# Every fourth low weight part of feed-forward made by an adding DMA instead of by VectorE

## The chip, the cores and the metric

The kernel runs on one core of one Trainium2 chip. The metric is the device time of one execution in microseconds; the time before is the median of three runs.

## The reference

A decoder block over 256 tokens of width 2048, all in float32: a conditioning vector gives shifts, scales and gates; a normalised and modulated input goes through one wide projection into gated linear attention (4 heads) and forgetting attention (16 heads), whose outputs are projected, gated, merged and added to x. The part that the change touches is the last:

```python
h2 = rms_norm(x, g_norm2[l]) * (1.0 + scale2) + shift2
x = x + gate2 * (jnp.square(jax.nn.relu(h2 @ w_ff1[l])) @ w_ff2[l])
return rms_norm(x, g_final)
```

with `w_ff1` of 2048 x 8192 and `w_ff2` of 8192 x 2048.

## The kernel before, in words

**Arithmetic.** A float32 product is made from three products in the format fp32r: each factor is split into a high part (itself, rounded) and a low part (what the rounding left out), and TensorE sums high x high, high x low and low x high. For the weights the high part `whi` is a copy by ScalarE that rounds (`hi`, L691 to L701), and the low part `wlo` is a subtraction by VectorE, raw minus `whi` (`lo`, L1156 to L1162).

**Units.** The weights are cut into units of 128 partitions x 2 x 512 float32, 512 KB. There are 608; `UNITS` (L59) numbers them in the order of their use. The sections are the three of the head, those of forgetting attention, of linear attention, of the mixing, of the output projection, and from `G_FF` = 352 on feed-forward: 256 units in four quarters (`it`) of 64, in each 32 units of `up` and 32 of `down`. `token_unit` (L1728) does one unit on TensorE: for two blocks of 128 tokens and two slices of the contraction three matmuls each, 12 in all, L1741.

**Buffers.** `raw` is a ring of 5 (`RING`), filled by DMAs that SP issues (`load`, L553; the issue is L577). Besides the units of the weights, pieces of `w_ada` ride in this ring up to the first part of feed-forward (L568). `whi` and `wlo` are rings of 4 (`WRING`), so that units of equal index modulo 4 share a buffer (`parts`, L505). All queues are written out by hand. In step g each of ScalarE and VectorE works on unit g + 3 (`LEAD`; `ahead`, L204).

**Semaphores.** ScalarE rounds unit g when its load has landed and TensorE has done unit g - 4 (`s_pe`), and raises `s_hi`. VectorE waits for `s_hi`, subtracts and raises `s_lo`, by one for each unit. TensorE waits for `s_lo` at g + 1 before the first matmul of unit g (L1731); SP waits for the same count before it loads into the raw buffer that unit g has left (L560).

**Other work in feed-forward.** In steps 8, 16, 24 and 32 of a quarter ScalarE takes a finished block out of PSUM with a relu (L1044) and VectorE squares it; in steps 11, 19, 27 and 35 TensorE transposes it by eight small matmuls (`turn`, L1717 to L1726); in steps 12, 20, 28 and 36 ScalarE and VectorE split it into its high and low part (L1050, L1586). VectorE adds the results of `down` to the residual stream (L1532, L1536).

**GpSimd.** It makes constants at the start, issues eight small DMAs of 4 and 8 KB (L645, L646), and computes the powers of the norms (L633, L637, L652). The last two powers (L652) belong to the final norm.

Of the kernel before, what the change touches and what calls it, by code (L numbers as in the profile page):

```python
# [6 lines left out]
ALU = mybir.AluOpType  # L7
# [186 lines left out]


NORM2_UNITS = (4, 9, 14)

# [32 lines left out]
def build(nc, x, c, w_ada, b_ada, g_norm1, w_in, w_gla_a_up, b_gla_a, g_gla_out, b_fox_f,  # L232
# [181 lines left out]

    s_hi = nc.alloc_semaphore("s_hi")
    s_lo = nc.alloc_semaphore("s_lo")
    s_pe = nc.alloc_semaphore("s_pe")
    s_bank = nc.alloc_semaphore("s_bank")
    s_bk = [nc.alloc_semaphore(f"s_bk{i}") for i in range(6)]
# [85 lines left out]
    def parts(g):  # L505

        if G_LAST <= g < NG - WRING:
            return hi_last[g - G_LAST], lo_last[g - G_LAST]
        return whi[g % WRING], wlo[g % WRING]
# [19 lines left out]
    with nc.Block() as block:  # L529


        @block.sync
        def _(sp):

            def load_bias(ag, col):
                if ag:
                    sp.wait_ge(s_ada, pieces_done(ag - 1, 0))
                for h in range(2):
                    sp.dma_start(bi[32 * h:32 * h + 1, :], b_ada[0:1, col + h * NB:col + h * NB + NB]).then_inc(s_bi, 16)

            def load_first(p):
                n, k = PIECE[p]
                col = n % 2 * 2 * NB + (D if n < 2 else 0)
                if p == P_0[n]:
                    if n:
                        sp.wait_ge(s_ada, 2 * (P_0[n - 1] + 1))
                    sp.dma_start(bih[0:1, :], b_ada[0:1, col:col + 2 * NB]).then_inc(s_bih, 16)
                if p >= FRING:
                    sp.wait_ge(s_ada, 2 * (p - FRING + 1))
                    sp.wait_ge(s_adp, pieces_pe(p - FRING))  # L550
                sp.dma_start(first[p % FRING][:], w_ada_v[:, k, col:col + 2 * NB]).then_inc(s_fraw[p % FRING], 16)

            def load(pos):  # L553
                kind, what = STREAM[pos]
                if kind == "a" and what[1] == 0:
                    load_bias(what[0], ADA_COL[what[0]])
                if pos >= RING:
                    kind_, what_ = STREAM[pos - RING]
                    if kind_ == "g":
                        sp.wait_ge(s_lo, what_ + 1)  # L560
                    elif kind_ == "w":
                        sp.wait_ge(s_wacc, 2 * what_ + 2)
                    else:
                        sp.wait_ge(s_ada, pieces_done(*what_))
                r = raw[pos % RING]
                if kind == "a":
                    m, k = what
                    sp.dma_start(r[:].rearrange("p k n -> p (k n)"), w_ada_v[:, k, ADA_COL[m]:ADA_COL[m] + 2 * NB]  # L568
                                 ).then_inc(s_raw[pos % RING], 16)
                elif kind == "w" and what >= UG:  # L570
                    both = w_in_v[:, what - UG, C_GV:C_GV + 2 * (C_GG - C_GV)].rearrange("p (a n) -> p a n", a=2)
                    sp.dma_start(r[:], both[:, :, 0:NB]).then_inc(s_raw[pos % RING], 16)
                else:
                    parts = source(what if kind == "g" else UNIT[("fq", 0), what])
                    n = NB // len(parts)
                    for a, src in enumerate(parts):
                        sp.dma_start(r[:, :, a * n:a * n + n], src).then_inc(s_raw[pos % RING], 16)  # L577

            sp.dma_start(x_in[:], x_v).then_inc(s_x, 16)
            sp.wait_ge(s_init, 1)  # L580
            loaded = 0
            for p in range(PIECES):
                load_first(p)
                while loaded < LOADED[p]:
                    load(loaded)
                    loaded += 1
            for pos in range(loaded, len(STREAM)):
                if pos == G_FOX + 4:

                    sp.wait_ge(s_zero, 1)  # L590
                    sp.dma_start(small[:, :, 0:RANK], w_in_v[:, :, C_LOW:C_LOW + RANK]).then_inc(s_small, 16)
                    sp.dma_start(small[:, :, 32:32 + FH], w_in_v[:, :, C_FL:C_FL + FH]).then_inc(s_small, 16)  # L592
                load(pos)

            for t in range(TT):
                for h, done in enumerate((s_ya, s_yo)):
                    half = slice(h * (D // 2), (h + 1) * (D // 2))
                    sp.wait_ge(done, t + 1 if h == 0 else 2 * t + 2)
                    sp.dma_start(out_v[:, t, half], xl[:, t, half]).then_inc(s_out, 16)
            sp.wait_ge(s_out, 16 * 2 * TT)  # L600


        @block.gpsimd
        def _(pool):
            nc.gpsimd.memset(bih[:], 0.0).then_inc(s_init, 1)
            nc.gpsimd.memset(ident[:], 0.0)
            nc.gpsimd.memset(ones[:], 1.0).then_inc(s_ones, 1)
            nc.gpsimd.memset(neghalf[:], -0.5)
            nc.gpsimd.memset(mhi[:], BIG)
            nc.gpsimd.memset(mlo[:], -BIG)  # L610
            nc.gpsimd.memset(tri[:], 1.0)
            nc.gpsimd.memset(tri16[:], 1.0 / TAU)
            nc.gpsimd.memset(fm[:], 0.0)
            nc.gpsimd.memset(am[:], 0.0)
            nc.gpsimd.memset(gl[:], 1.0).then_inc(s_init, 1)
            pool.wait_ge(s_init, 2)

            nc.gpsimd.affine_select(out=ident[:], in_=ident[:], compare_op=ALU.not_equal, fill=1.0, base=0,
                                    pattern=[[-1, P]], channel_multiplier=1).then_inc(s_ident, 1)
            nc.gpsimd.memset(small[:], 0.0).then_inc(s_zero, 1)  # L620
            for t_ in (mhi, mlo, tri, tri16):
                nc.gpsimd.affine_select(out=t_[:], in_=t_[:], compare_op=ALU.is_ge, fill=0.0, base=0,
                                        pattern=[[1, P]], channel_multiplier=-1).then_inc(s_mask, 1)
            for b in (0, 2):
                nc.gpsimd.affine_select(out=fm[:, b * P:b * P + P], in_=fm[:, b * P:b * P + P],
                                        compare_op=ALU.is_ge, fill=-1e30, base=0,
                                        pattern=[[-1, P]], channel_multiplier=1).then_inc(s_mask, 1)
            pool.wait_ge(s_mask, 6)
            nc.gpsimd.memset(tri16[0:CH, CH:P], 0.0).then_inc(s_mask, 1)

            def norm_pow(r):
                pool.wait_ge(s_nms, r + 1)
                nc.gpsimd.tensor_tensor(nst[:, 2, :], nst[:, 1, :], neghalf[:], ALU.pow).then_inc(s_ny, 1)  # L633

            def gla_pow(h):
                pool.wait_ge(s_gms, h + 1)
                nc.gpsimd.tensor_tensor(nst[:, 2, :], nst[:, 1, :], neghalf[:], ALU.pow).then_inc(s_gy, 1)  # L637

            norm_pow(0)

            pool.wait_ge(s_fcd, 4)
            for a in range(2):
                own = slice(a * FH // 2, (a + 1) * FH // 2)
                for row, src in ((32 * a, nch), (32 * a + 1, ncl)):
                    nc.gpsimd.dma_start(ncrow[row:row + 1, :, 0:P], src[own, 0:P]).then_inc(s_rowcum, 16)  # L645
                    nc.gpsimd.dma_start(ncrow[row:row + 1, :, P:3 * P], src[own, :]).then_inc(s_rowcum, 16)  # L646
            for h in range(4):
                gla_pow(h)
            norm_pow(1)
            for t in range(TT):  # L650
                pool.wait_ge(s_nms, 3 + t)
                nc.gpsimd.tensor_tensor(nst[:, 2, t:t + 1], nst[:, 1, t:t + 1], neghalf[:, 0:1], ALU.pow  # L652
                                        ).then_inc(s_ny, 1)
# [3 lines left out]
        def _(act):  # L657
# [33 lines left out]
            def hi(g):  # L691

                if g >= NG:
                    return
                act.wait_ge(s_raw[POS_G[g] % RING], landed(POS_G[g]))
                if g >= NG - WRING:

                    act.wait_ge(s_pe, g - 2 * WRING + 1)
                elif g >= WRING and g < G_LAST:
                    act.wait_ge(s_pe, g - WRING + 1)  # L700
                nc.scalar.activation(parts(g)[0][:], raw[POS_G[g] % RING][:], ACT.Copy).then_inc(s_hi, 1)  # L701

            act.wait_ge(s_nr, 3)
            nc.scalar.activation(xn[:, 1, :], x_in[:, 1, :], ACT.Copy, scale=nst[:, 5, 1:2]).then_inc(s_xna, 1)
# [370 lines left out]
        def _(dve):  # L1075
# [79 lines left out]

            def lo(g):  # L1156

                if g >= NG:
                    return
                dve.wait_ge(s_hi, g + 1)  # L1160
                top, rest = parts(g)
# [470 lines left out]
        def _(pe):  # L1632
# [95 lines left out]
            def token_unit(name, u, src, ready=None, rows=range(TT)):  # L1728
                g = UNIT[name, u]
                top, rest = parts(g)  # L1730
                pe.wait_ge(s_lo, g + 1)  # L1731
                for t in rows:
                    if u == 0:
                        bank_free(name, t)
# [339 lines left out]
```

## Time and profile before

| | us |
|---|---|
| median of three runs | 1881.63 |
| lowest and highest | 1879.43, 1885.69 |
| span of the profiled execution | 1879.2 |
| TensorE busy in it | 1835.8 |
| VectorE busy | 1231.8 |
| ScalarE busy | 848.2 |
| GpSimd busy | 17.7 |

Of the profiled execution the span from the first to the last instruction is given, and no time of its own beside it. PE is TensorE, PEld its loads of the stationary operand, DVE VectorE, ACT ScalarE, POOL GpSimd; SPq is the queue of SyncE that issues DMAs. Busy time of an engine says how much it works, not whether anybody waits for it; for that there are the waits and the chain that ended last.

### The profile page before, as it was taken

What the parts mean: (1) busy time and instruction counts of PE and PEld (TensorE: products, weight loads), DVE (VectorE), ACT (ScalarE), POOL (GpSimd) and SP (SyncE); (2) the same over time, 40 slices, a digit from 0 to 9 for tenths busy, and PEclk for the clock granted to TensorE, in tenths of its full rate; (3) what the DMA queues carried; (4) which work ended last, traced back from release to release, by engine and by line L of the source; (5) the groups of instructions that cost most, each with busy time, mean ns of one, the idle gap of its engine ahead of it and who ended that gap; (6) DMA issues with size and microseconds to landing.
All of it is one profiled execution on the core that took longest, in us unless ns stands there. A gap on an engine that the chain in (4) does not pass through costs nothing.

```text
span 1879.2 us, 21671 instructions
## 1 busy us (share of the span) xinstructions
PE 1835.8 (98%) x8351; PEld 1485.1 (79%) x8351; DVE 1231.8 (66%) x1368; ACT 848.2 (45%) x1075; POOL 17.7 (1%) x40
## 2 busy tenths in 40 slices
PE   6998999999999999999999998999999999999998
PEld 3666888888888888888888886888888888888886
DVE  6996666666666667666576777775555555555555
ACT  4444545455544554344444444443444344434443
POOL 1000000000000000000000000000000000000000
PEclk8999999999999999999999998999999999999999
DMA  9998899899997987998899784886666666666663
GB/s 382 399 318 250 215 218 278 240 232 256 206 206 236 214 246 232 250 260 295 276 256 266 254 282 156 286 279 201 192 190 180 194 198 181 190 192 191 188 190 123
DMA packets 214767, 441.50 MB, mean 235 GB/s; under 512 B 18437, under 2 KB 34917, under 8 KB 214282
## 3 DMA queue, kind: packets, MB, share of 16 engines
q1 hardware_dynamic: 213272, 436.57, 78.5%
q10 hardware_dynamic: 1138, 3.50, 0.5%
q8 instruction: 67, 1.10, 0.2%
q14 instruction: 34, 0.28, 0.0%
q0 software_dynamic: 256, 0.05, 0.0%
HBM read 437.92 MB, written 2.10 MB: 234 GB/s over the span
## 4 chain that ended last, share of the span: by engine, by line
PE 89%; DVE 2%; DMA 1%; issue 1%; SPq 1%; ACT 0%; POOL 0%; POOLq 0%; DVEq 0%
PE ps L1741 82%; PE ps L1725 1%; DMA raw<-in_w_in 1%; PE ps L1845 1%; DVE wlo L1162 1%; DVE acch L1134 0%; SPq L592 0%; PE ps L1897 0%; PE ps L1649 0%; PE ps L1651 0%; DVE xT L1567 0%; PE ps L1842 0%; ACT whi L701 0%; PE ps L1854 0%; DVE obT L1571 0%
## 5 line engine op out<-in xcount | busy, mean ns | idle before, releaser
L1162 DVE TENSOR_TENSOR wlo<-raw,whi 128x1024 fp32r<-128x1024 f32 x604 | 738.3, 1224 | 587.4 <-ACT whi L701 585.3
L701 ACT ACTIVATE whi<-raw 128x1024 fp32r<-128x1024 f32 x604 | 639.5, 1060 | 935.9 <-PE ps L1741 719.3
L1741 PE MATMUL ps<-whi,hT 128*128 128x512 f32 x2304 | 742.9, 397 | 5.0 <-DVE wlo L1162 4.6
L1741 PEld LDWEIGHTS ps<-whi,hT 128*128 128x128 f32 x2304 | 435.1, 189 | 114.0 <-DVE wlo L1162 13.1
L1741 PE MATMUL ps<-wlo,hT 128*128 128x512 f32 x1152 | 450.6, 391 | 0.0
L1741 PE MATMUL ps<-whi,obT 128*128 128x512 f32 x1280 | 403.9, 393 | 3.9 <-DVE wlo L1162 2.7
L1741 PE MATMUL ps<-whi,oaT 128*128 128x512 f32 x1248 | 389.0, 390 | 0.0
L1741 PEld LDWEIGHTS ps<-whi,obT 128*128 128x128 f32 x1280 | 242.0, 189 | 56.3 <-DVE wlo L1162 4.2
L1741 PEld LDWEIGHTS ps<-whi,oaT 128*128 128x128 f32 x1248 | 234.3, 188 | 48.9 <-issue 0.5
L1741 PEld LDWEIGHTS ps<-wlo,hT 128*128 128x128 f32 x1152 | 217.7, 189 | 45.4 <-issue 2.2
L1741 PE MATMUL ps<-wlo,obT 128*128 128x512 f32 x640 | 250.5, 391 | 0.0
L1741 PE MATMUL ps<-wlo,oaT 128*128 128x512 f32 x624 | 242.8, 389 | 0.0
L1273 DVE SCALAR_TENSOR_TENSOR acc<-raw,cond,acc 128x1024 f32<-128x1024 f32 x120 | 153.3, 1277 | 0.7 <-DMA raw<-in_w_ada 0.4
L1741 PEld LDWEIGHTS ps<-wlo,obT 128*128 128x128 f32 x640 | 121.1, 189 | 25.1 <-issue 0.5
L1741 PEld LDWEIGHTS ps<-wlo,oaT 128*128 128x128 f32 x624 | 117.2, 188 | 24.6 <-issue 0.5
L1134 DVE SCALAR_TENSOR_TENSOR acch<-first,cond,acch 128x1024 f32<-128x1024 f32 (+1 forms) x60 | 64.1, 1068 | 8.5 <-DMA first<-in_w_ada 5.1
L1532 DVE TENSOR_TENSOR rt<-ps,gate 128x512 f32<-128x512 f32 x40 | 27.4, 684 | 8.4 <-PE ps L1741 8.4
L1699 PE MATMUL ps<-first,cond 128*1 128x512 f32 x48 | 26.9, 660 | 4.1 <-DMA first<-in_w_ada 4.1
L1536 DVE TENSOR_TENSOR xl<-xl,rt 128x512 f32<-128x512 f32 x40 | 27.7, 693 | 4.2
L1580 DVE TENSOR_TENSOR t<-t 128x512 f32<-128x512 f32 x32 | 20.6, 684 | 0.0
L1586 DVE TENSOR_TENSOR oaT<-ps,oaT 128x512 fp32r<-128x512 f32 x32 | 20.5, 682 | 0.0
L1225 DVE SCALAR_TENSOR_TENSOR accv<-raw,modc,accv 128x1024 f32<-128x1024 f32 x15 | 19.1, 1275 | 0.0
(234 smaller groups left out, 783.7 us busy)
## 6 DMA issues: line engine op xcount, KB each, us to landing
raw<-in_w_ff SPq DMA_DIRECT2D x256, 512.0 KB, 4.2
raw<-in_w_in SPq DMA_DIRECT2D x248, 512.0 KB, 6.7
raw<-in_w_ada SPq DMA_DIRECT2D x128, 512.0 KB, 5.2
first<-in_w_ada SPq DMA_DIRECT2D x64, 512.0 KB, 10.2
raw<-in_w_in SPq DMA_DIRECT2D x64, 256.0 KB, 6.1
raw<-in_w_proj_fox SPq DMA_DIRECT2D x32, 512.0 KB, 5.7
raw<-in_w_proj_gla SPq DMA_DIRECT2D x32, 512.0 KB, 5.6
raw<-in_w_out SPq DMA_DIRECT2D x32, 512.0 KB, 5.0
```

The costliest lines, as they stand in the source:

```text
L701: nc.scalar.activation(parts(g)[0][:], raw[POS_G[g] % RING][:], ACT.Copy).then_inc(s_hi, 1)
L1134: V.scalar_tensor_tensor(b[:, c], a[:, c], cond[:, k:k + 1], bih[:] if k == 0 else b[:, c], ALU.mult, ALU.add).then_inc(s_ada, 2)
L1162: V.tensor_tensor(rest[:], raw[POS_G[g] % RING][:], top[:].bitcast(F32), ALU.subtract).then_inc(s_lo, 1)
L1225: V.scalar_tensor_tensor(acc_, w, col, acc_, ALU.mult, ALU.add).then_inc(s_wacc, inc)
L1273: V.scalar_tensor_tensor(acc[:], raw[pos % RING][:].rearrange("p k n -> p (k n)"), cond[:, k:k + 1], acc[:], ALU.mult, ALU.add).then_inc(s ...
L1532: V.tensor_tensor(rt[:, t, :], ps[bank(name, t)][:], gate[:, cols], ALU.mult).then_inc(s_bk[bank(name, t)], 1)
L1536: V.tensor_tensor(xl[:, t, cols], xl[:, t, cols], rt[:, t, :], ALU.add).then_inc(s_x2, 1)
L1580: V.tensor_tensor(t5[:, t, :], t5[:, t, :], t5[:, t, :], ALU.mult).then_inc(s_act, 1)
L1586: V.tensor_tensor(oaT[:, 4 * b:4 * b + 4, 1, t * P:t * P + P], ps[bank(("up", n), t)][:].rearrange("p (k n) -> p k n", k=4), oaT[:, 4 * b: ...
L1699: T.matmul(ps[6][0:1, :], cond[:, k:k + 1], first[p % FRING][:, 0:NB], start=(p == p0), stop=(p == p1)).then_inc(s_adp, 1)
L1725: i = T.transpose(ps[bank(name, t)][:, k * P:k * P + P], src[:, t, k * P:k * P + P], ident[:])
L1741: i = T.matmul(ps[bank(name, t)][:], src[:, kt, hl, tk], w[:, k, :], start=(kt == 0 and n == 0), stop=(kt == KT - 1 and n == 2))
```

## The change

For every fourth unit of feed-forward (unit numbers that leave 2 when divided by 4, from 358 to 590) ScalarE makes, behind the rounded copy, a second one with scale -1, which it writes into the unit's `wlo` buffer. GpSimd waits for it and issues a DMA that reads the unit's weights from memory again and adds them onto that buffer, which then holds the raw value minus the rounded one. VectorE leaves these units out. TensorE waits for the DMA's semaphore in these units, and for a count of `s_lo` that leaves them out in the others; SP takes the raw buffer of such a unit as free after the negated copy.

```diff
--- before.py
+++ after.py
@@ -194,6 +194,21 @@
 
 
 NORM2_UNITS = (4, 9, 14)
+
+
+
+FOLD = [g for g in range(G_FF + 6, NG - 2 * UG) if g % 4 == 2]
+FOLD_N = {g: n for n, g in enumerate(FOLD)}
+
+
+def folded(g):
+
+    return sum(f <= g for f in FOLD)
+
+
+def own_lo(g):
+
+    return g + 1 - folded(g)
 
 
 
@@ -414,6 +429,8 @@
 
     s_hi = nc.alloc_semaphore("s_hi")
     s_lo = nc.alloc_semaphore("s_lo")
+    s_neg = nc.alloc_semaphore("s_neg")
+    s_fold = nc.alloc_semaphore("s_fold")
     s_pe = nc.alloc_semaphore("s_pe")
     s_bank = nc.alloc_semaphore("s_bank")
     s_bk = [nc.alloc_semaphore(f"s_bk{i}") for i in range(6)]
@@ -557,7 +574,10 @@
                 if pos >= RING:
                     kind_, what_ = STREAM[pos - RING]
                     if kind_ == "g":
-                        sp.wait_ge(s_lo, what_ + 1)
+                        if what_ in FOLD_N:
+                            sp.wait_ge(s_neg, FOLD_N[what_] + 1)
+                        else:
+                            sp.wait_ge(s_lo, own_lo(what_))
                     elif kind_ == "w":
                         sp.wait_ge(s_wacc, 2 * what_ + 2)
                     else:
@@ -647,6 +667,9 @@
             for h in range(4):
                 gla_pow(h)
             norm_pow(1)
+            for n, g in enumerate(FOLD):
+                pool.wait_ge(s_neg, n + 1)
+                nc.gpsimd.dma_start(parts(g)[1][:], source(g)[0], accum_op=ALU.add).then_inc(s_fold, 16)
             for t in range(TT):
                 pool.wait_ge(s_nms, 3 + t)
                 nc.gpsimd.tensor_tensor(nst[:, 2, t:t + 1], nst[:, 1, t:t + 1], neghalf[:, 0:1], ALU.pow
@@ -699,6 +722,8 @@
                 elif g >= WRING and g < G_LAST:
                     act.wait_ge(s_pe, g - WRING + 1)
                 nc.scalar.activation(parts(g)[0][:], raw[POS_G[g] % RING][:], ACT.Copy).then_inc(s_hi, 1)
+                if g in FOLD_N:
+                    nc.scalar.activation(parts(g)[1][:], raw[POS_G[g] % RING][:], ACT.Copy, scale=-1.0).then_inc(s_neg, 1)
 
             act.wait_ge(s_nr, 3)
             nc.scalar.activation(xn[:, 1, :], x_in[:, 1, :], ACT.Copy, scale=nst[:, 5, 1:2]).then_inc(s_xna, 1)
@@ -1155,7 +1180,7 @@
 
             def lo(g):
 
-                if g >= NG:
+                if g >= NG or g in FOLD_N:
                     return
                 dve.wait_ge(s_hi, g + 1)
                 top, rest = parts(g)
@@ -1728,7 +1753,10 @@
             def token_unit(name, u, src, ready=None, rows=range(TT)):
                 g = UNIT[name, u]
                 top, rest = parts(g)
-                pe.wait_ge(s_lo, g + 1)
+                if g in FOLD_N:
+                    pe.wait_ge(s_fold, 16 * (FOLD_N[g] + 1))
+                else:
+                    pe.wait_ge(s_lo, own_lo(g))
                 for t in rows:
                     if u == 0:
                         bank_free(name, t)
```

## Rows read from the trace of the kernel before

**Rows 1.** The page: busy time, and the busy tenths of 40 slices.

```profile
PE 1835.8 (98%) x8351; PEld 1485.1 (79%) x8351; DVE 1231.8 (66%) x1368; ACT 848.2 (45%) x1075; POOL 17.7 (1%) x40
...
PE   6998999999999999999999998999999999999998
...
DVE  6996666666666667666576777775555555555555
ACT  4444545455544554344444444443444344434443
```

**Rows 2.** The page: the chain that ended last, by line.

```profile
PE ps L1741 82%; PE ps L1725 1%; DMA raw<-in_w_in 1%; PE ps L1845 1%; DVE wlo L1162 1%; DVE acch L1134 0%; SPq L592 0%; PE ps L1897 0%; PE ps L1649 0%; PE ps L1651 0%; DVE xT L1567 0%; PE ps L1842 0%; ACT whi L701 0%; PE ps L1854 0%; DVE obT L1571 0%
```

**Rows 3.** Stretches of feed-forward: us, busy (count) by engine, granted clock, DMA share, GB/s.

```profile
1190.00:1250.00 60.00, 60.00 (x274) 49.86 (x273) 43.77 (x43) 28.25 (x34) 0.00 (x0) 1.00 0.83 276
...
1400.00:1600.00 200.00, 200.00 (x904) 166.04 (x903) 109.91 (x108) 86.05 (x92) 0.00 (x0) 1.00 0.64 189
```

**Rows 4.** 1190 to 1850 us: waits (total, times, longest), then groups of instructions.

```profile
ACT whi L701 <- PE ps L1741: 368.9, 231, 2.6
DVE wlo L1162 <- ACT whi L701: 273.0, 212, 2.4
ACT whi L701 <- DMA raw<-in_w_ff: 4.0, 3, 2.1
...
L1162 DVE TENSOR_TENSOR wlo<-raw,whi 128x1024 fp32r<-128x1024 f32 x235 | 287.9, 1225 | 273.1 <-ACT whi L701 273.0
L701 ACT ACTIVATE whi<-raw 128x1024 fp32r<-128x1024 f32 x236 | 250.2, 1060 | 373.0 <-PE ps L1741 368.9 <-DMA raw<-in_w_ff 4.0
```

**Rows 5.** Timeline from 1500 us: start, us, engine, line, operation [idle before].

```profile
1500.12 0.19 PEld L1741 LDWEIGHTS ps<-wlo,oaT 128*128 128x128 f32 x1
1500.34 0.39 PE L1741 MATMUL ps<-wlo,oaT 128*128 128x512 f32 x1
...
1500.57 0.62 PE L1741 MATMUL ps<-whi,oaT 128*128 128x512 f32 x2
...
1501.05 1.06 ACT L701 ACTIVATE whi<-raw 128x1024 fp32r<-128x1024 f32 x1 [1.66 <-PE ps L1741]
...
1502.14 1.23 DVE L1162 TENSOR_TENSOR wlo<-raw,whi 128x1024 fp32r<-128x1024 f32 x1 [1.50 <-ACT whi L701]
...
1503.77 1.06 ACT L701 ACTIVATE whi<-raw 128x1024 fp32r<-128x1024 f32 x1 [1.66 <-PE ps L1741]
...
1508.73 0.62 PE L1741 MATMUL ps<-whi,oaT 128*128 128x512 f32 x2
```

**Rows 6.** Timeline of ACT: a rounding and what runs directly behind it.

```profile
1536.41 1.06 ACT L701 ACTIVATE whi<-raw 128x1024 fp32r<-128x1024 f32 x1 [1.66 <-PE ps L1741]
1537.38 1.07 ACT L1044 ACTIVATE t<-ps 128x512 f32<-128x512 f32 x2
```

**Rows 7.** Loads of L577, 1400 to 1850 us, and the page's DMA totals.

```profile
DMA to landing us min/median/max: 3.6/3.9/6.0
...
DMA packets 214767, 441.50 MB, mean 235 GB/s; under 512 B 18437, under 2 KB 34917, under 8 KB 214282
```

**Rows 8.** POOL's timeline, and the landing of its small DMAs (tile ncrow).

```profile
208.18 0.52 POOL L646 DMA_DIRECT2D ncrow<-nch  x1
...
1143.72 0.69 POOL L633 TENSOR_TENSOR nst<-nst,neghalf 128x2 f32<-128x2 f32 x1 [413.29 <-DVE nst L1114]
1861.67 0.55 POOL L652 TENSOR_TENSOR nst<-nst,neghalf 128x1 f32<-128x1 f32 x1 [717.26 <-DVE nst L1114]
...
DMA to landing us min/median/max: 3.2/3.8/4.0
```

**Rows 9.** All DMA issues: KB each, median us to landing.

```profile
raw<-in_w_in SPq DMA_DIRECT2D x248, 512.0 KB, 6.7
```

**Rows 10.** DMA in the first 50 us: GB/s of 40 slices.

```profile
GB/s 0 97 244 419 420 432 397 419 419 419 413 410 403 400 419 416 413 403 393 419 395 400 400 395 398 398 410 398 405 392 401 406 397 400 410 383 393 415 405 388
```

**Rows 11.** The chain from 1480 to 1560 us: start, us, what.

```profile
1544.48 0.87 PE ps L1725 x8
```

## The prediction

> **What bounds the kernel now.** I read the views from the coarse to the fine. First the page's busy shares and its 40 slices [rows 1]: TensorE is busy 98% of the span and VectorE 66%; the reader is to see that in the last 15 slices, feed-forward, PE stays at 9 while DVE falls to 5 and ACT is at 3 to 4. Then the chain that ended last [rows 2]: 82% of the span is the weight matmuls of L1741, while the low parts of L1162 are near 0%. Then the stretches of feed-forward [rows 3]: PE is busy in every microsecond (PE's column equals the length of the stretch) at a granted clock of 1.00, which is the 2.4 GHz level. Then the waits there [rows 4]: DVE waits 273.0 us for ACT's rounded part, ACT waits 368.9 us for PE to free a buffer, and PE waits for no other engine. So VectorE's work in this stage is off the path. Taking it away cannot shorten anything by itself; the question is only whether the new way delivers each low part in time.
>
> **How much time a low part has.** One unit is 12 matmuls. In the timeline [rows 5] the rounding activations start at 1501.05 and 1503.77, so a unit lasts 2.72 us. The pair of matmuls at 1500.57 is the last of one unit and the first of the next, the second of them starting 0.23 later, at 1500.80 (its end at 1500.96, 0.09 before the activation, is what releases ACT). The buffer freed there serves the unit three places behind the one just begun, whose first matmul is the second of the pair at 1508.73, that is 1508.96; a stationary load starts 0.22 ahead of its matmul (1500.12 and 1500.34), and it stands behind the same wait. So from 1501.05 the low part has until 1508.74, 7.7 us. Today it needs 2.3: 1.06 for ACT, 1.23 for DVE until 1503.37 [rows 5]. That leaves 5.4 us unused.
>
> **The change part by part.**
> *Count.* The changed units run from feed-forward's sixth to before its last sixteen, every fourth: 59.
> *Removed:* 59 subtractions of 1.225 us [rows 4], 72 us of VectorE. Worth nothing: the cover is the 273.0 us in which DVE idles behind ACT in this stage.
> *Added on ACT:* 59 activations of 1.06 us [rows 4], 63 us, in 368.9 us of idle time. One directly behind another starts 0.97 after it (1536.41 to 1537.38 [rows 6]), so the negated copy runs from 1502.02 to 1503.08. What is queued behind it on ACT is the rounding of the next unit, due at 1503.77: not delayed. The relu and transposed-block work of ACT comes in steps 8, 12 and so on, the negated copies in steps 3, 7, 11 and so on, ahead of their rounding's next step: no collision. Price zero.
> *Moved on SP:* the buffer of a changed unit is released by the negated copy at 1503.08 instead of by the subtraction at 1503.37, so SP's next load goes out 0.3 us earlier. Loads land in 3.9 us [rows 7] and have several units of lead, ACT waits for them only 4.0 us in 660 [rows 4]: worth nothing. The other units' release count skips the changed ones; DVE's order is otherwise the same.
> *Added on POOL:* 59 issues. POOL does nothing between 1143.7 and 1861.7 us [rows 8], so nothing is queued in front of them, and the last power of the norm comes after the last of them. An issue of the existing small DMAs takes 0.52 us [rows 8]; 256 rows of 2 KB instead of a few must cost more to describe, no row shows how much, and I put 0.5 us on top.
> *Added as transfer, and this is the step that decides:* the 512 KB are read again from memory and added onto 512 KB in SBUF. It has from 1503.11 (DVE too starts 0.03 after ACT's end) to 1508.74: **5.6 us**. No row shows an adding transfer. Bounds: from below, a plain 512 KB load from SP lands in 3.6 us at best, 3.9 in the median [rows 7]; it cannot be quicker than that. From above, a plain load in the input projections lands in 6.7 us in the median [rows 9]; with a second pass over the data (1.25 us, below) and 0.5 for the issue that is 8.5. Between: POOL's DMAs of 4 to 8 KB take 3.8 us from issue to landing [rows 8], which is nearly all latency. To it come two passes over 512 KB (the source and the old content of the destination), at the 419 GB/s of saturated slices [rows 10] 1.25 us each, and the 0.5 of the longer issue: 3.8 + 2.5 + 0.5 = **6.8 us**. I take this value, since it starts from the only row of POOL's own queue; that the engines are shared with the loads speaks for more, that part of a pass hides in the latency for less, and I let these cancel.
> *The wait on PE:* late by 6.8 - 5.6 = 1.2 us. Queued behind it on PE are only the matmuls themselves, so each delay is paid in full and then does not grow: the next changed unit's buffer is freed by the end of this one, with three undelayed units between. In 16 of the 59 (the fourteenth, 22nd, 30th and 38th unit of each quarter) eight transposes, 0.87 us [rows 11], lie in the interval and give them 6.5 us. Sum: 43 x 1.2 + 16 x 0.3 = 56 us.
> *DMA load:* 59 more transfers of 0.52 MB are 31 MB on 441 [rows 7]; in this stage 189 GB/s become some 237, or more if the second read counts. The loads get slower but have slack.
>
> The profiled execution has a span of 1879.2 us; it is 2.4 below the 1881.63 of the median and within the range of the runs, so I add the sum to the median: 1881.6 + 56 = 1938.
>
> Weighed against a rule. The row of POOL's queue gives 3.8 us for almost no data, and so 6.8 for this transfer. The Trainium skill, DMA: Bandwidth & Descriptors, section "Anatomy of one DMA — SWDGE (gpsimd) path", fits 2.0 us plus the bytes at 436 GB/s, an estimate of 3.2 us for 512 KB; by it the sum of the change would be zero. Rows 8 do not agree with its fixed part, 3.8 us for 8 KB.
>
> **Rivals.**
> A, *in time, no change* (the other side: not slower). Mechanism: the latency of 3.8 us overlaps the data, the destination's pass runs beside the source's, so 3.8 + 1.25 + 0.5 = 5.5 us or less, just inside the 5.6. It decides at 5.6 us from issue to landing. For it: a plain load of 512 KB takes 3.9 us [rows 7], hardly more than POOL's 8 KB at 3.8, so latency hides data, or SP's queue is quicker. Against it: if it is the queue, nothing is hidden. Time: 1882, chance 0.28. The Trainium skill's fit named above is this rival, and would make it safe by over 2 us; no run here shows it yet.
> B, *the DMA engines become the bound.* The stage uses 64% of them for 189 GB/s [rows 3], so one load costs 0.64 x 2.72 = 1.74 us of all engines; four units last 10.9 us and use 7.0. If an adding transfer costs as much as three plain ones (two reads, one sum and write) the group needs 12.2 us, more than it has; transfers then queue and land after some 9.5 us, 3.9 late: 43 x 3.9 + 16 x 3.0 = 216, a time of 2098. For it: the first 60 us of the stage already show a share of 0.83. Against: the same engines move 419 GB/s when asked, so the share overstates the use. Chance 0.15.
> C, *faster*: only if PE's pace, 2.72 us for 12 matmuls, were slowed by VectorE's traffic in SBUF. The pace does not follow DVE's load: 274 matmuls in 60 us, 4.6 per us, with DVE at 73%, and 904 in 200, 4.5 per us, with DVE at 55% [rows 3]. Chance 0.02, some 1870. That the change does not do what it says I see no room for: 59 subtractions are gone or they are not.
>
> **How the numbers follow.** Forecast, late by 0.2 to 3 us each: chance 0.55, its own range 1890 to 2040 (the upper bound, 8.5 us, is 2.9 late: 43 x 2.9 + 16 x 2.0 = 157). A measurement of this kernel can tell 0.3%, 6 us, from no change; that is 0.1 us per changed unit. Slower: 0.55 + 0.15 = 0.70; same 0.28; faster 0.02. The range takes in A whole and the forecast's bounds: 1876 to 2040; above it lies B.
>
> **What would show it.** In the profile after: DVE busy near 1160 us, ACT near 911, both certain. PE idle in front of L1741 for a wait on the adding DMA, about 43 times 1.2 us, each in a unit of index 2 modulo 4, shortest after the transposes. POOL's issues near 1.0 us, their landing near 6.8. Wrong if the landing is under 5.6 (A), or if ACT too begins to wait for raw loads and the DMA share is over 0.9 (B); the term most open is the landing time.

## The result, and the profile after

The changed kernel takes 2016.53 us in the median of four runs (2010.76 to 2018.9), the kernel before 1883.18 in the runs beside it: a ratio of 1.070 (95% interval 1.0679 to 1.0721). It is 133 us slower. The direction was forecast and the time lies in the range; the size, 56 us, was less than half of the measured one.

The page of the kernel after: busy times, busy tenths in 40 slices, and the chain that ended last by line. Line numbers have moved: L1769 is the weight matmul (L1741 before), L724 the rounding, L726 the negated copy, L672 the adding DMA, L1187 the subtraction.

```profile
PE 1881.6 (93%) x8351; PEld 1500.4 (74%) x8351; DVE 1159.0 (57%) x1309; ACT 903.9 (45%) x1134; POOL 88.2 (4%) x99
...
PE   6999999999999999999999878988988898889988
...
DVE  6986767666676676666677755533333333334435
...
PEclk8998999999999999999999889999999999999999
...
PE ps L1769 55%; DMA wlo<-in_w_ff 21%; ACT whi L724 3%; ACT wlo L726 3%; DMA raw<-in_w_in 2%; DVE wlo L1187 1%; PE ps L1750 1%; PE ps L1873 1%; DVE acch L1159 0%; SPq L612 0%; PE ps L1925 0%; PE ps L1674 0%; DVE xT L1592 0%; PE ps L1870 0%; PE ps L1882 0%
```

VectorE's 1159 us answer to 1231.8 of before [rows 1]: the subtractions are gone. ScalarE is busy 903.9 us, a little under the 911 that the prediction called certain: a negated copy directly behind a rounding adds 0.96 us, not 1.06. PE no longer stands at 9 in the last 15 slices. The clock row still does, in tenths; what it hides comes below. In the chain the weight matmuls fall from 82% to 55%, and what took their place is the transfer `wlo<-in_w_ff`, 21%.

The waits from 1190 to 1980 us (total, times, longest):

```profile
POOL wlo L672 <- ACT wlo L726: 706.2, 58, 16.7
DVE wlo L1187 <- ACT whi L724: 472.7, 155, 9.3
ACT whi L724 <- PE ps L1769: 450.3, 236, 6.4
PEld ps L1769 <- DMA wlo<-in_w_ff: 109.0, 58, 3.3
PE ps L1769 <- DMA wlo<-in_w_ff: 84.4, 55, 2.8
```

Before, PE waited for no other engine here [rows 4]. Now its loads of the stationary operand wait for the adding DMA 58 times, in every changed unit of the stretch, 1.9 us in the mean (a small part of which, in the account below, is no delay). ScalarE waits for a raw load only once here, for 0.2 us.

One turn of the new loop, the chain from 1408 us (start, us, what):

```profile
1407.15 1.06 ACT whi L724
1408.21 0.96 ACT wlo L726
1409.16 0.29 issue
1409.45 6.72 DMA wlo<-in_w_ff
1416.18 0.04 issue
1416.22 3.04 PE ps L1769 x12
1419.26 0.02 issue
```

Rounding, negated copy, 0.29 us until POOL starts, 6.72 us until the data has landed, one unit of 12 matmuls, and the next rounding: it is a closed loop of 12.2 us here, where four units and the transposes among them need 11.8.

DMA from 1190 to 1980 us: queue, packets, MB, share of the 16 engines; issues with us to landing:

```profile
q1 hardware_dynamic: 66983, 132.84, 52.1%
q0 software_dynamic: 15776, 30.41, 22.7%
...
raw<-in_w_ff SPq DMA_DIRECT2D x240, 512.0 KB, 4.4
wlo<-in_w_ff POOLq DMA_DIRECT2D x58, 512.0 KB, 7.5
```

The landing is 7.5 us in the median (6.8 in the prediction). An adding transfer holds the engines for 22.7% of 790 us by 58, 3.09 us; a load for 52.1% of 790 by 255, 1.61. Together that is 0.75 of the stretch.

The second part of the loss is in the clock. One of PE's waits, and four stretches of 2 us (busy time and count of PE, PEld, DVE, ACT, POOL; granted clock; DMA share; GB/s):

```profile
1441.91 0.19 PEld L1769 LDWEIGHTS ps<-whi,obT 128*128 128x128 f32 x1 [2.52 <-DMA wlo<-in_w_ff]
```

```profile
1440.00:1442.00 2.00, 0.09 (x1) 0.09 (x1) 1.00 (x1) 0.96 (x1) 0.00 (x0) 1.00 1.01 330
1442.00:1444.00 2.00, 2.00 (x6) 1.57 (x7) 0.22 (x1) 0.00 (x0) 0.00 (x0) 0.57 0.65 184
1444.00:1446.00 2.00, 2.00 (x7) 1.57 (x6) 0.00 (x0) 0.00 (x0) 0.00 (x0) 0.58 0.57 208
1446.00:1448.00 2.00, 2.00 (x15) 1.72 (x14) 0.00 (x0) 1.38 (x2) 0.00 (x0) 1.00 0.00 0
```

PE's load waited 2.5 us for the DMA (its matmuls stood still for 2.1), and when PE began again at 1441.9 it was granted 0.57 and 0.58, that is mostly the 1.2 GHz level: 13 matmuls in 4 us instead of 18. By the clock records of the trace there are 13 such stretches between 1195 and 1870 us, 44 us in sum, against none before, and half of that is lost: 22 us. Before each the matmuls had stood still for 1.9 to 2.8 us. Not every such wait ends so: after the 2.3 us that end at 1794.7 the clock stayed at its upper level.

The account for the profiled execution, 137.9 us longer than before: PE's wait for the DMA, 117.7 us with the first changed unit, less some 0.14 a time that the load of the stationary operand has as its place before the matmul anyway, 109; the clock 22. That is 131 of 138. Of the 7 us left, 5.3 lie ahead of the first changed unit: the matmul that starts at 1150 us before starts 5.3 us later in this execution. The change has no part in them.

### The profile page after: what moved, and what is told of

Its sections match the earlier page's. It is cut to its first block, busy times and chain, and to the rows that moved or that the text cites. A ratio compares the mean times of both kernels' runs of the same rounds, so it can differ in the third digit from the quotient of the medians.

```text
span 2017.1 us, 21730 instructions
## 1 busy us (share of the span) xinstructions
PE 1881.6 (93%) x8351; PEld 1500.4 (74%) x8351; DVE 1159.0 (57%) x1309; ACT 903.9 (45%) x1134; POOL 88.2 (4%) x99
## 4 chain that ended last, share of the span: by engine, by line
PE 61%; DMA 23%; ACT 6%; DVE 2%; issue 2%; SPq 1%; POOL 0%; ACTq 0%; POOLq 0%; DVEq 0%
PE ps L1769 55%; DMA wlo<-in_w_ff 21%; ACT whi L724 3%; ACT wlo L726 3%; DMA raw<-in_w_in 2%; DVE wlo L1187 1%; PE ps L1750 1%; PE ps L1873 1%; DVE acch L1159 0%; SPq L612 0%; PE ps L1925 0%; PE ps L1674 0%; DVE xT L1592 0%; PE ps L1870 0%; PE ps L1882 0%
## 5 line engine op out<-in xcount | busy, mean ns | idle before, releaser
L1187 DVE TENSOR_TENSOR wlo<-raw,whi 128x1024 fp32r<-128x1024 f32 x545 | 666.3, 1224 | 797.0 <-ACT whi L724 794.9
L724 ACT ACTIVATE whi<-raw 128x1024 fp32r<-128x1024 f32 x604 | 639.3, 1059 | 1016.3 <-PE ps L1769 816.3
L1769 PE MATMUL ps<-whi,hT 128*128 128x512 f32 x2304 | 745.7, 398 | 5.2 <-DVE wlo L1187 4.9
L1769 PEld LDWEIGHTS ps<-whi,hT 128*128 128x128 f32 x2304 | 437.0, 190 | 115.5 <-DVE wlo L1187 13.3
L1769 PE MATMUL ps<-whi,obT 128*128 128x512 f32 x1280 | 417.8, 401 | 45.4 <-DMA wlo<-in_w_ff 43.1
L1769 PE MATMUL ps<-whi,oaT 128*128 128x512 f32 x1248 | 407.8, 403 | 49.1 <-DMA wlo<-in_w_ff 49.1
L1769 PE MATMUL ps<-wlo,hT 128*128 128x512 f32 x1152 | 452.2, 393 | 0.0
L1769 PEld LDWEIGHTS ps<-whi,obT 128*128 128x128 f32 x1280 | 245.6, 192 | 111.0 <-DMA wlo<-in_w_ff 56.3
L1769 PEld LDWEIGHTS ps<-whi,oaT 128*128 128x128 f32 x1248 | 241.5, 194 | 112.7 <-DMA wlo<-in_w_ff 61.4
L1769 PE MATMUL ps<-wlo,obT 128*128 128x512 f32 x640 | 254.0, 397 | 0.0
L1769 PEld LDWEIGHTS ps<-wlo,hT 128*128 128x128 f32 x1152 | 218.7, 190 | 45.7 <-issue 2.2
L1769 PE MATMUL ps<-wlo,oaT 128*128 128x512 f32 x624 | 249.3, 400 | 0.0
L1769 PEld LDWEIGHTS ps<-wlo,obT 128*128 128x128 f32 x640 | 122.9, 192 | 25.0 <-issue 0.5
L1769 PEld LDWEIGHTS ps<-wlo,oaT 128*128 128x128 f32 x624 | 120.9, 194 | 24.8 <-issue 0.2
L672 POOL DMA_DIRECT2D wlo<-in_w_ff x59 | 70.4, 1193 | 730.4 <-ACT wlo L726 730.4
L726 ACT ACTIVATE wlo<-raw 128x1024 fp32r<-128x1024 f32 x59 | 61.5, 1043 | 0.0
L657 POOL TENSOR_TENSOR nst<-nst,neghalf 128x2 f32<-128x2 f32 x4 | 5.2, 1289 | 513.0 <-DVE nst L1116 513.0
```

The costliest lines, as they stand in the source:

```text
L672: nc.gpsimd.dma_start(parts(g)[1][:], source(g)[0], accum_op=ALU.add).then_inc(s_fold, 16)
L726: nc.scalar.activation(parts(g)[1][:], raw[POS_G[g] % RING][:], ACT.Copy, scale=-1.0).then_inc(s_neg, 1)
L1187: V.tensor_tensor(rest[:], raw[POS_G[g] % RING][:], top[:].bitcast(F32), ALU.subtract).then_inc(s_lo, 1)
L1769: i = T.matmul(ps[bank(name, t)][:], src[:, kt, hl, tk], w[:, k, :], start=(kt == 0 and n == 0), stop=(kt == KT - 1 and n == 2))
```

## The experiments

Twelve kernels, each compared with the kernel before on the same chip. The table has the ratio of each, its interval, and the landing of the transfer, median over the whole run. The kernel before ran at 1883.2 to 1885.5 us beside them (medians), so a difference of 2 us between two rows says nothing.

| run | us | ratio to before | landing, us |
|---|---|---|---|
| the changed kernel | 2016.5 | 1.070 (1.068 to 1.072) | 7.5 |
| neg_first | 2005.9 | 1.064 (1.061 to 1.067) | 8.3 |
| low_last | 1922.3 | 1.019 (1.017 to 1.022) | 7.9 |
| both_moves | 1921.2 | 1.019 (1.017 to 1.021) | 8.8 |
| early_two | 1905.1 | 1.011 (1.009 to 1.013) | 7.1 |
| pool_plain | 1904.0 | 1.010 (1.008 to 1.012) | 5.5 |
| act_plain | 1917.8 | 1.018 (1.015 to 1.021) | 5.8 |
| pool_add_f32 | 2016.8 | 1.070 (1.067 to 1.072) | 7.6 |
| hold_load | 1943.0 | 1.030 (1.027 to 1.033) | 6.1 |
| early_after_pieces | 1882.0 | 0.9995 (0.9986 to 1.0004) | 7.6 |
| neg_first_hold | 1926.2 | 1.023 (1.021 to 1.024) | 6.7 |
| every_eighth | 1965.7 | 1.045 (1.042 to 1.047) | 7.7 |
| early_one | 1909.1 | 1.014 (1.011 to 1.016) | 8.5 |

### Giving the low part more time

**neg_first.** In a changed unit the negated copy comes ahead of the rounded one; SP's wait moves to the rounded one, which is now the last reader of the raw buffer.

```diff
+                if g in FOLD_N:
+                    nc.scalar.activation(parts(g)[1][:], raw[POS_G[g] % RING][:], ACT.Copy, scale=-1.0).then_inc(s_neg, 1)
                 nc.scalar.activation(parts(g)[0][:], raw[POS_G[g] % RING][:], ACT.Copy).then_inc(s_hi, 1)
-                if g in FOLD_N:
-                    nc.scalar.activation(parts(g)[1][:], raw[POS_G[g] % RING][:], ACT.Copy, scale=-1.0).then_inc(s_neg, 1)
...
                         if what_ in FOLD_N:
-                            sp.wait_ge(s_neg, FOLD_N[what_] + 1)
+                            sp.wait_ge(s_hi, what_ + 1)
...
                 if g in FOLD_N:
+                    pe.wait_ge(s_hi, g + 1)
                     pe.wait_ge(s_fold, 16 * (FOLD_N[g] + 1))
```

> Edit: in a changed unit ScalarE makes the negated copy ahead of the rounded one, so the adding DMA is asked for 0.97 us earlier and nothing else moves. Theory (lateness of a transfer of fixed length, landing 7.5 us after its issue): of the 46 waits that the trace shows, each less the 0.25 us that it has anyway, 1.77 us in the mean, what is over 0.97 stays, 0.86 us each, 51 us in sum, and with fewer long waits the low-clock stretches fall from 14 to some 5: 1945 us (1935 to 1960). Rival (the DMA engines are the bound, 7.0 of 10.9 us plus the adding transfers): an earlier issue only queues longer, 2005 us or more.

Measured 2005.9 us: 10 us gained where 70 were expected, and the landing rose by 0.8 us, nearly the whole of the 0.97 gained. Neither theory has this: it is the rival's time, but not its mechanism, since hardly a raw load was late (ScalarE waited for three of them, 4.4 us).

**low_last.** In a changed unit TensorE does the eight matmuls with the rounded part first.

```diff
                 if g in FOLD_N:
-                    pe.wait_ge(s_fold, 16 * (FOLD_N[g] + 1))
+                    pe.wait_ge(s_hi, g + 1)
+                    for low in (False, True):
+                        if low:
+                            pe.wait_ge(s_fold, 16 * (FOLD_N[g] + 1))
+                        for t in rows:
...
+                                for hl, w in ((0, rest),) if low else ((0, top), (1, top)):
```

> Edit: in a changed unit TensorE does the eight matmuls with the rounded part first and waits for the adding DMA only before the four with the low part, 1.81 us later. Theory (lateness): only what is over 1.8 us of each wait stays, 18 us in sum, no low-clock stretches: 1900 us (1890 to 1912). Rival (DMA engines the bound): 1990 us or more. The same landing time of 7.5 us by the theory, a longer one by the rival.

Measured 1922.3 us: 94 of the 133 us gained, some nine times what the other move brought, though it is only twice the time. It is above the theory's range (1890 to 1912) and far from the rival. This lead is on PE's side, behind the transfer, and the landing follows it by only 0.4 us (7.9). Its wait from 1310 to 1800 us:

```profile
PEld ps L1767 <- DMA wlo<-in_w_ff: 24.6, 28, 1.8
```

That is 0.9 us in 28 of 42 units. No stretch of low clock is left between 1195 and 1870 us, so the 22 us of the clock are among the 94.

**both_moves.** The two together.

> Edit: the two moves together, 2.8 us more time for each low part. Theory: all waits but that of the first unit gone, 1886 us (1882 to 1892). Rival (DMA engines the bound): 1980 us or more, with ACT waiting for raw loads.

Measured 1921.2 us, no better than low_last alone and outside the theory's range (1882 to 1892), with a landing of 8.8: again 0.9 of the 0.97 us of the earlier negated copy was given back by a later landing.

**early_two.** The low parts of the changed units get two buffers of their own, on the tile hT, whose last reader is the output projection; the negated copy is made behind the rounding of the unit two places ahead.

```diff
+    flo = [at(f"flo{i}", [P, KU, NB], offset[0] - 32768 + 4096 * i, F32R) for i in range(2)]
...
-                if g in FOLD_N:
-                    nc.scalar.activation(parts(g)[1][:], raw[POS_G[g] % RING][:], ACT.Copy, scale=-1.0).then_inc(s_neg, 1)
+                if g + 2 in FOLD_N:
+                    f = g + 2
+                    act.wait_ge(s_raw[POS_G[f] % RING], landed(POS_G[f]))
+                    nc.scalar.activation(parts(f)[1][:], raw[POS_G[f] % RING][:], ACT.Copy, scale=-1.0).then_inc(s_neg, 1)
```

> Edit: the changed units' low parts get two buffers of their own on the tile hT, which is dead in feed-forward, and ScalarE makes the negated copy two units earlier (some 5.4 us), as soon as the load has landed. Theory: lateness gone, the time is that of the kernel before within 0.3%, 1883 us; VectorE's 72 us bring nothing. Rival 1 (DMA engines the bound): over 1950 us. Rival 2 (the freed VectorE is worth something once nothing is late): 1870 us or less.

Measured 1905.1 us, between theory and rival 1. The stretches tell why (columns as above):

```profile
1190.00:1310.00 120.00, 106.53 (x462) 84.15 (x461) 62.14 (x62) 50.95 (x58) 10.68 (x9) 0.97 0.87 262
1310.00:1800.00 490.00, 490.00 (x2208) 406.59 (x2207) 215.72 (x221) 251.56 (x266) 52.46 (x44) 1.00 0.86 236
```

From 1310 us on PE is busy in every microsecond again, as before [rows 3], beside 44 adding transfers: in time they cost nothing. All of the loss lies ahead of it, where pieces of `w_ada` share the raw ring. The waits of 1190 to 1310 us:

```profile
ACT whi L725 <- DMA raw<-in_w_ff: 27.7, 7, 5.0
ACT flo L729 <- DMA raw<-in_w_ff: 25.4, 8, 4.4
```

The early copy waits in ScalarE's queue for a raw load, and the roundings behind it wait too.

### What of the transfer is dear

**pool_plain.** The POOL DMA does not add, and goes to a scratch tile. The kernel leaves out the low part of the changed units: TensorE takes the negated copy for it.

```diff
-                nc.gpsimd.dma_start(parts(g)[1][:], source(g)[0], accum_op=ALU.add).then_inc(s_fold, 16)
+                nc.gpsimd.dma_start(scr[n % 2][:], source(g)[0]).then_inc(s_fold, 16)
```

> Edit: the POOL DMA of each changed unit is a plain load of the same 512 KB into a scratch tile on hT, without the addition; TensorE waits for it at the same place. Left out: the low parts of the changed units stay negated copies. In the kernel after, an adding transfer holds the 16 engines for 3.09 us (22.7% of 790 us by 58) and a plain load for 1.63. Theory (the addition is dear in the engines, and the plain part is not): landing 1.4 to 2 us shorter, 5.5 to 6 us, time 1890 to 1915 us. Rival (POOL's queue is what is dear, its issue of 1.19 us and its latency): landing about 7 us, 1975 us or more.

**act_plain.** The same plain load, from ScalarE's queue, with the same left out.

```diff
+                    act.wait_ge(s_neg, FOLD_N[g] + 1)
+                    act.dma_start(scr[FOLD_N[g] % 2][:], source(g)[0]).then_inc(s_fold, 16)
```

> Edit: the same plain load into the scratch tile, issued by ScalarE's queue behind the negated copy instead of by POOL. Left out: the same as in the run with POOL's plain load. Theory: another 1.0 us or so shorter (no descriptors written by POOL), landing 4.3 to 5 us, in time: 1883 to 1890 us. Rival (contention with the loads of SP is all): the same time as with POOL's plain load.

**pool_add_f32.** The negated copy and the adding DMA go to a float32 tile. TensorE does not read it, so the low part of the changed units is left out here too.

```diff
-                    nc.scalar.activation(parts(g)[1][:], raw[POS_G[g] % RING][:], ACT.Copy, scale=-1.0).then_inc(s_neg, 1)
+                    nc.scalar.activation(scr[FOLD_N[g] % 2][:], raw[POS_G[g] % RING][:], ACT.Copy, scale=-1.0).then_inc(s_neg, 1)
...
+                nc.gpsimd.dma_start(scr[n % 2][:], source(g)[0], accum_op=ALU.add).then_inc(s_fold, 16)
```

> Edit: the negated copy and the adding DMA go to a float32 scratch tile on hT instead of the fp32r tile wlo, so the DMA adds but does not change the type; TensorE waits for it at the same place. Left out: the low parts of the changed units are not made. Theory (the addition is the price): as the kernel after, landing 7.3 to 7.7, 2000 to 2025 us. Rival (the change of type is the price): as with POOL's plain load, under 1950 us.

DMA of pool_plain from 1190 to 1880 us:

```profile
q0 software_dynamic: 8208, 29.89, 11.0%
...
scr<-in_w_ff POOLq DMA_DIRECT2D x57, 512.0 KB, 5.5
```

And of pool_add_f32 in the same stretch:

```profile
q0 software_dynamic: 14099, 27.17, 23.4%
...
scr<-in_w_ff POOLq DMA_DIRECT2D x51, 512.0 KB, 7.6
```

The addition is the price. Without it the transfer holds the engines for 11.0% of 690 us by 57, 1.33 us, with it for 23.4% by 51, 3.17 (and it goes in 144 packets instead of some 270, 8208 by 57), and it lands 2.1 us sooner, 0.47 of them in the issue (0.72 us for the plain one in POOL's timeline, 1.19 for the adding one); the time falls by 113 of the 133 us. The change of type costs nothing: 2016.8 with float32 and 2016.5 with fp32r. POOL's queue is no dearer than ScalarE's either. There theory and rival both failed: act_plain lands at 5.8, not 4.3 to 5, and is 14 us slower than pool_plain; PE waits 34.0 us for its transfers, where it waits 18.6 for those of pool_plain. The issue itself is shorter (0.47 us), and the plain load takes 272 packets from this queue (15504 by 57). Why it lands later was not followed up.

### What makes the landing follow the issue

**hold_load.** SP waits for the adding DMA before it fills the raw buffer of that unit.

```diff
                             sp.wait_ge(s_neg, FOLD_N[what_] + 1)
+                            sp.wait_ge(s_fold, 16 * (FOLD_N[what_] + 1))
```

> Edit: SP waits for the adding DMA to land before it loads into the raw buffer of that unit; the loads behind it wait too. The first run with the negated copy ahead gained 10 us where 70 were expected, because the transfer then took 8.3 us. Theory now (a load that SP issues beside it goes first and shares the engines, so the landing depends on when the loads fall): landing 5.7 to 6.3 us, time 1895 to 1930 us. Rival (the landing is the transfer's own): 7.5 us as before and 2015 us; a rise above that would be ACT waiting for the held loads.

```profile
PEld ps L1770 <- DMA wlo<-in_w_ff: 51.5, 48, 3.1
ACT whi L725 <- DMA raw<-in_w_ff: 50.0, 12, 8.2
```

The landing is 6.1, as the theory has it, and PE's wait for it halves. The time, 1943.0, is above the theory's 1930: the held loads now come late for ScalarE, 50.0 us in 12 waits.

So a load of SP beside the adding transfer makes it land later. In the changed kernel both are let go by the same event, the end of the negated copy: in its timeline, first the queue of SP, then POOL:

```profile
1409.18 0.37 SPq L597 DMA_DIRECT2D raw<-in_w_ff  x1
```

```profile
1409.45 1.20 POOL L672 DMA_DIRECT2D wlo<-in_w_ff  x1 [11.25 <-ACT wlo L726]
```

In neg_first the load goes on the end of the rounding, after the start of POOL's issue, and yet the load's data goes first. The timeline of neg_first, of ACT, POOL and SP:

```profile
1408.51 1.06 ACT L725 ACTIVATE wlo<-raw 128x1024 fp32r<-128x1024 f32 x1 [3.12 <-PE ps L1770]
...
1409.47 1.04 ACT L726 ACTIVATE whi<-raw 128x1024 fp32r<-128x1024 f32 x1
...
1409.87 1.19 POOL L672 DMA_DIRECT2D wlo<-in_w_ff  x1 [11.14 <-ACT wlo L725]
```

```profile
1410.54 0.37 SPq L597 DMA_DIRECT2D raw<-in_w_ff  x1
```

Its DMA queues from 1411 to 1413.5 us, and then from 1414 to 1416.5 (packets, MB, share):

```profile
q1 hardware_dynamic: 149, 0.31, 65.9%
```

```profile
q0 software_dynamic: 234, 0.48, 105.1%
q1 hardware_dynamic: 42, 0.06, 6.8%
```

149 packets of the load and none of the adding DMA in the first, although POOL's issue had begun 0.67 us before SP's; then the adding DMA has nearly the whole of the engines.

The packets of the trace say why the load is first (medians behind the pieces). A load of SP has its first packet 1.01 us after its issue. The adding DMA, with the load held (hold_load), has its first 1.9 us after the start of POOL's issue, which itself takes 1.19. So a load that SP issues up to 0.9 us later is ahead of it all the same: in the changed kernel the load's data starts 0.7 us after POOL, in neg_first 1.7, and in both it was first in all of the 41 changed units behind the pieces. The adding DMA's own first packet then comes 2.5 us after POOL's start in the changed kernel and 4.2 in neg_first. That is where the 0.97 us went; the transfer then meets less of the next load, so that the landing is 0.8 us later and not 1.7.

That the second queue then waits for nearly all of the first is seen, not explained. The Trainium skill, DMA: Bandwidth & Descriptors, section "Queues, rings and completion order", says that each engine goes round the queues packet by packet, and drains a packet of typically 9 to 17 descriptors from one before it turns to the next. The profile counts 272 packets for an adding transfer (15776 by 58 above), 17 for each of the 16 engines. If what the profile calls a packet is a descriptor of the page, a transfer's share of an engine is one turn, and these stretches agree with the page; if it is not, they disagree. No run here tells.

**neg_first_hold.** The earlier copy together with the held load.

> Edit: the negated copy ahead of the rounded one, and SP holds its next load until the adding DMA has landed. Alone the first gave 10 us, the second 73. Theory (the first failed because the transfer then met the load that SP issues on the rounded copy's end, and waited behind it): with the load held the landing stays at 6.1 us and the 0.97 us count in full, PE's waits on it fall from 51.5 us to under 20: 1910 us (1900 to 1925), the rest being ACT's waits for held loads. Rival (an earlier issue never helps, the engines are full): 1943 us or more.

Measured 1926.2, just outside the theory's range: 17 us under hold_load, where 33 were expected, and the landing is 6.7. The earlier issue does help once the load is out of its way (17 of 33, against 10 of 70), but the landing again grew, by 0.6. The mechanism is supported, not complete.

### Where it costs something even in time

**early_after_pieces.** As early_two, the first changed unit is 402.

```diff
-FOLD = [g for g in range(G_FF + 6, NG - 2 * UG) if g % 4 == 2]
+FOLD = [g for g in range(G_FF + 50, NG - 2 * UG) if g % 4 == 2]
```

> Edit: the version with own buffers and a negated copy two units earlier, but the first changed unit is 402 instead of 358, so none of the 48 left stands beside the pieces of w_ada that ride in the raw ring. In the run with all 59, POOL's issues came every 10.9 or 11.8 us from 1310 us on, which is PE's own pace, and every 13 to 15 us before. Theory: the 22 us that it cost all lie in that stretch, where the DMA engines move some 267 GB/s and raw loads come late: 1884 us, within 0.3% of before. Rival (the adding transfers cost something everywhere, the stretch only shows it): 1898 us or more.

```profile
1190.00:1310.00 120.00, 120.00 (x539) 98.86 (x538) 80.06 (x79) 53.90 (x59) 2.47 (x2) 1.00 0.81 260
1310.00:1600.00 290.00, 290.00 (x1309) 240.67 (x1308) 128.03 (x131) 149.46 (x159) 31.05 (x27) 1.00 0.87 237
1600.00:1840.00 240.00, 240.00 (x1080) 199.12 (x1080) 109.17 (x112) 122.81 (x135) 23.75 (x20) 1.00 0.85 233
```

Measured 1882.0 us, a ratio of 0.9995 (0.9986 to 1.0004). 48 adding transfers that land after 7.6 us, as late as in the changed kernel, cost nothing, and the 59 us of subtractions that VectorE is spared (48 by 1.224) bring nothing. This is the clearest run of the study: the price was never the transfer, but its lateness.

**early_one.** As early_two, one unit early instead of two.

> Edit: all 59 changed units with own buffers, the negated copy one unit earlier (2.7 us) instead of two. With two units the 20 us lay before 1310 us, where ScalarE's early copy waited 25.4 us for raw loads and its roundings another 27.7. Theory (the early copy stands in ScalarE's queue in front of roundings and waits for a load that the ring, shared with the pieces, brings late): with one unit less of lead these waits fall under 15 us, and 2.7 us cover most of the lateness of 1.8 us: 1892 us (1886 to 1898). Rival (the DMA engines are full in that stretch): 1905 us as before, with PE or ACT waiting there for transfers as long as in the version with two.

The waits from 1190 to 1310 us, and the stretches:

```profile
ACT flo L729 <- DMA raw<-in_w_ff: 7.0, 6, 1.8
...
ACT whi L725 <- DMA raw<-in_w_ff: 4.6, 2, 2.5
```

```profile
1190.00:1310.00 120.00, 114.06 (x506) 91.80 (x506) 64.17 (x65) 57.28 (x62) 11.22 (x10) 0.99 0.92 272
1310.00:1800.00 490.00, 479.78 (x2138) 391.85 (x2137) 207.86 (x212) 242.13 (x256) 51.26 (x43) 1.00 0.85 229
```

Measured 1909.1 us, above the theory's 1898. ScalarE's waits for raw loads before 1310 us fell from 53.1 to 11.6 us, as the theory has it, and PE's idle time ahead of 1310 us fell with them, from 13.5 of the 120 us (106.53 busy in early_two) to 5.9. What it had wrong is the rest: the landing rose to 8.5 us, one unit of lead no longer covered it, and PE idles 10.2 us of the 490 behind 1310 us, where it idled none with two units of lead.

**every_eighth.** 29 changed units (the expectation counts 30).

```diff
-FOLD = [g for g in range(G_FF + 6, NG - 2 * UG) if g % 4 == 2]
+FOLD = [g for g in range(G_FF + 6, NG - 2 * UG) if g % 8 == 2]
```

> Edit: every eighth unit instead of every fourth, 30 changed units. Theory (a price for each, no bound by the engines' mean load): 30 of 59 of 133 us, 68 us, 1952 us (1940 to 1962). Rival (the mean load of the DMA engines decides): far less than half, under 1915 us.

```profile
PEld ps L1769 <- DMA wlo<-in_w_ff: 62.3, 26, 3.9
```

Measured 1965.7 us, above both ranges: 82 us for 29 units, 2.8 each, against 2.25 each for 59. Half the adding transfers do not cost less each, so the mean load of the engines does not decide; the rival is out. That each costs more has in part a reason that the expectation overlooked: units that leave 2 when divided by 8 are never the ones with the eight transposes in their interval (the 14th, 22nd, 30th and 38th of a quarter), so none has their 0.87 us. It is not all: by the trace the same 28 units behind the first wait 2.2 us each in the changed kernel and 2.4 here. Why was not followed up.

## Why the prediction was right in its direction and wrong in its size

*What bounds the kernel* held: PE does, VectorE's work in this stage is worth nothing (early_after_pieces), the question is lateness alone.

*The interval of 5.6 us* was right but for its start (5.6 is the time between the end of ScalarE's copy and PE's need). The prediction let POOL start 0.03 us after ScalarE's end, as DVE does; it starts 0.29 after. That leaves 5.4.

*The transfer, 3.8 + 2.5 + 0.5 = 6.8 us,* is the step that failed first: it landed after 7.5. Of its terms the issue was near (1.19 against 1.02). Two passes at 419 GB/s were too few: the addition holds the engines for 3.09 us instead of 2.5. Even so the transfer alone, with SP's load held, lands in 6.1 us (hold_load), 0.7 less than the sum, so the other terms were too large by more than that. What the prediction got wrong is that it let the sharing with SP's loads cancel against what hides in the latency: the first is worth 1.4 us (7.5 less 6.1), the second 0.7. That the sum came as near as 6.8 is in part luck, two errors of opposite sign.

*SP's queue* was priced at nothing, "0.3 us earlier". The prediction looked at what that load needs and not at what it does to others: it is the load that the adding transfer waits behind. Whether the 0.3 us matter no run tells; neg_first lets the load go later, and the landing is later still.

*The wait of 1.2 us* was then 2.1 (the trace has 2.15 in the 42 units of the stretch without transposes). In the 16 with transposes it is shorter, as forecast, but 1.15 instead of 0.3 (1.43 us at 1416.2 without them, 0.74 at 1428.6 with them). Some 0.14 us of each is no delay.

*The clock* is not in the sum at all. Behind some of the waits PE's granted clock was at its lower level, and that cost 22 us.

Put together: 0.7 for the landing and 0.26 for POOL's start, by 59, are 57 us; with the 56 forecast that is 113, where the account of the trace has 109; with the 22 of the clock it is 135, for 133 measured. The way from ScalarE's end to the landing was mis-sized by 0.96 us, a seventh of it; but the loss is its excess over the interval of 5.6, and that nearly doubled.

Rival A fell at 7.5 us. The fit of the Trainium skill that spoke for it (DMA: Bandwidth & Descriptors, section "Anatomy of one DMA — SWDGE (gpsimd) path"; by it an estimate of 3.2 us for 512 KB) is 2.3 below even POOL's plain load, which landed in 5.5 beside SP's loads. Rival B is not what happened in the changed kernel, whose DMA share is 0.75 and whose ScalarE hardly waits for a load: an adding transfer costs the engines as much as two plain ones (3.09 us against 1.61), not three; something like it shows beside the pieces when the copies come early (early_two, early_one). Rival C is out by early_after_pieces: a VectorE with less work does not speed PE.

## What to carry to other kernels

Before work is moved from an engine to a DMA, set the time that the result has against the landing that the queue really shows, with the other loads beside it, and expect an error of that difference, not of the landing. If it is late, first move the consumer (the matmuls that do not need the result go first: 94 of 133 us) or give the result a buffer of its own; an earlier issue alone can be eaten by a load that another queue issues shortly before or after it. And if the engine relieved was not the bound, even a perfect version gains nothing.

## What the runs showed of the hardware

- A DMA that adds holds the 16 engines 3.1 us for 512 KB in rows of 2 KB, a plain one from the same queue 1.33, and it lands 2 us later (7.5 against 5.5). Into fp32r or float32 is the same (7.5 and 7.6).
- A load of SP has its first packet 1.01 us after its issue, POOL's adding DMA 1.9 us after the start of its own with no load beside it. A transfer that POOL issued 0.3 us after a load of SP, or 0.67 before it, had nearly all of its data moved behind that of the load.
- POOL's issue starts 0.29 us after the activation that it waits for, VectorE's instruction 0.03 us after.
- After 13 of the changed kernel's waits, in each of which the matmuls stood still for 1.9 to 2.8 us, the granted clock was at its lower level for the next few microseconds (0.57 and 0.58 in two stretches of 2 us); in low_last, where PE's loads of the stationary operand wait 0.9 us in the mean behind 1310 us and 1.8 at most (its matmuls 1.3), it never was.
